# Half of the low-half subtractions of U moved from VectorE to GpSimd in the last expert stage

## The reference, cut to what matters

```python
def chunk(args):
    xc, ic, gc = args
    u = jnp.take(u_tab, ic, axis=0)
    act = jax.nn.gelu(jnp.einsum('chkd,cd->chk', u, xc), approximate=False)
    return jnp.einsum('chk,chkd->cd', gc * act, jnp.take(v_tab, ic, axis=0))
```

## Time and profile before

| | us |
|---|---|
| median of 3 runs | 2609.61 (2608.39 to 2610.11) |
| the profiled execution, device time | 2614.08 |
| span of its profile, first to last instruction | 2612.3 |
| PE busy | 2377.7 (91%) |
| DVE busy | 1766.5 (68%) |
| POOL busy | 908.3 (35%) |
| ACT busy | 777.9 (30%) |

### The profile page before, as it was taken

How to read it: one execution, slowest core, us unless ns; L and a number is a source line. 1 busy time by engine, 2 the same in 40 slices (tenths; PEclk the granted TensorE clock), 3 DMA queues, 4 the chain that set the end, 5 groups by cost and what they waited for, 6 DMA issues and landing times.

```text
span 2612.3 us, 34126 instructions
## 1 busy us (share of the span) xinstructions
PE 2377.7 (91%) x12686; PEld 1830.0 (70%) x12686; DVE 1766.5 (68%) x3612; ACT 777.9 (30%) x1388; POOL 908.3 (35%) x650
## 2 busy tenths in 40 slices
PE   5988899969999999999978778998899999999995
PEld 4756689859757766666657567987795777666662
DVE  1345479978668777677754456897884886777775
ACT  2354442113225422122243444311231452222221
POOL 3400360431221154555444205217113114555552
PEclk7999989989999999999989888999899999999997
DMA  6455334886799899999934702279669998999993
GB/s 262 139 179 193 131 112 129 312 313 226 281 316 317 281 366 370 366 364 366 366 115 147 209 25 85 92 269 360 207 223 344 313 320 316 377 378 356 384 369 133
DMA packets 219907, 679.71 MB, mean 260 GB/s; under 512 B 32384, under 2 KB 63152, under 8 KB 219232
## 3 DMA queue, kind: packets, MB, share of 16 engines
q1 hardware_dynamic: 142912, 396.42, 43.2%
q0 software_dynamic: 76832, 281.11, 28.7%
HBM read 658.87 MB, written 18.56 MB: 259 GB/s over the span
## 4 chain that ended last, share of the span: by engine, by line
PE 60%; DVE 15%; DMA 13%; ACT 4%; issue 3%; POOL 3%; SPq 1%; ACTq 0%; DVEq 0%
PE ps L1056 15%; PE ps L737 9%; PE ps L739 9%; PE ps L738 9%; DMA ring<-in_u 8%; PE ps L1033 7%; DVE arena L2033 3%; POOL arena L655 3%; PE ps L1012 2%; PE ps L919 2%; DMA arena<-gelu_half 2%; DMA arena<-in_u_rows,arena 2%; PE ps L900 2%; DVE arena L1927 1%; ACT u_split L1324 1%
## 5 line engine op out<-in xcount | busy, mean ns | idle before, releaser
L1056 PE MATMUL ps<-ring,arena 128*128 128x512 f32 x1264 | 568.9, 595 | 20.7 <-DVE arena L1981 20.6
L655 POOL DMA_INDIRECT arena<-in_u_rows,arena x256 | 294.0, 1148 | 782.6 <-DVE arena L2014 598.3
L655 POOL DMA_INDIRECT arena<-in_v,arena x256 | 355.8, 1390 | 353.8 <-DVE arena L2014 168.3
L1033 PE MATMUL ps<-arena,ring 128*128 128x256 f32 x2048 | 457.6, 382 | 1.1 <-ACT arena L1279 0.6
L1033 PEld LDWEIGHTS ps<-arena,ring 128*128 128x128 f32 x2048 | 386.5, 191 | 53.2 <-issue 1.9
L1056 PEld LDWEIGHTS ps<-ring,arena 128*128 128x128 f32 x1264 | 231.4, 190 | 268.8 <-issue 268.2
L615 POOL TENSOR_TENSOR ring_lo<-ring,ring_hi 128x1024 fp32r<-128x1024 f32 x84 | 216.4, 2588 | 415.5 <-ACT ring_hi L1158 415.5
L2014 DVE CUSTOM_DVE_ANT_0 arena<-arena 128x1024 f32<-128x1024 f32 x256 | 310.8, 1221 | 47.9 <-DMA arena<-in_u_rows,arena 47.5
L2033 DVE SCALAR_TENSOR_TENSOR arena<-arena 128x1024 f32<-128x1024 f32 x254 | 325.7, 1282 | 15.3 <-DMA arena<-in_v,arena 1.2
L737 PE MATMUL ps<-xs_high,u_split 128*128 128x256 f32 x1024 | 335.4, 328 | 0.1
L2003 DVE TENSOR_TENSOR u_split<-ring,u_split 128x1024 fp32r<-128x1024 f32 x128 | 156.7, 1224 | 218.4 <-ACT u_split L1324 218.4
(11 more groups left out here) (245 smaller groups left out, 3549.1 us busy)
## 6 DMA issues: line engine op xcount, KB each, us to landing
ring<-in_u SPq DMA_DIRECT2D x256, 512.0 KB, 6.3
ring<-in_v SPq DMA_DIRECT2D x256, 512.0 KB, 5.9
ring<-in_w_mod SPq DMA_DIRECT2D x80, 512.0 KB, 4.2
ring<-in_w_in SPq DMA_DIRECT2D x36, 512.0 KB, 3.3
ring<-in_w_q SPq DMA_DIRECT2D x32, 512.0 KB, 3.2
gelu_half<-arena SPq DMA_DIRECT2D x120, 128.0 KB, 4.7
arena<-gelu_half SPq DMA_DIRECT2D x120, 128.0 KB, 4.7
arena<-in_w_mod SPq DMA_DIRECT2D x16, 512.0 KB, 19.8
```

The costliest lines, as they stand in the source:

```text
L655: pool.indirect_dma_start(row[at], None, table, bass.IndirectOffsetOnAxis(where[:, k:k + 1], axis=0)).then_inc(sem(f"row_in{at}"), 16)
L1033: ins = mm(hidden_bank(b), slot[c % RING][:, P * k:P * k + P], HFS[:, k, :], start=(k == 0), stop=(k == KC - 1))
L1056: ins = mm(ps[:, t + 3 * q, :], GL[:, b % GLS, P * t - P:P * t], slot[c % RING][:, 512 * q:512 * q + 512], start=(b == MIDDLE[0]), stop=(b ...
```

## The change

The low halves of blocks 67, 69, ..., 127 are made by POOL. These are 31 blocks in each layer and 62 in all; the even ones, and block 65, stay on DVE. POOL's gathers are counted by r from 0 to 255 in the order of use. If S is the number of the first row of step b - 3, in which DVE made the low half of block b, POOL now makes it directly ahead of gather S + 4. `BESIDE` holds this place for each block.

```diff
+SHARED = range(SPILL + 3, KEYS, 2)
+BESIDE = {}
+for b in SHARED:
+    BESIDE.setdefault(min(HALF + sum(len(d) + len(s) for d, s in LATE[:b - 3 - SPILL]) + 4, 2 * P - 1), []).append(b)
...
+            def low_u(l, b):
+
+                c = u_chunk(l, b)
+                pool.wait_ge(sem("us_hi"), since("us_hi", l) + b - SPILL + 1)
+                pool.tensor_tensor(u_half(b, 1), slot[c % RING], f32(u_half(b, 0)), ALU.subtract).then_inc(used(c % RING), 1)
+
             def experts(l):
...
+                    for b in BESIDE.get(r, ()):
+                        low_u(l, b)
                     gather(l, r)
...
-                    if b + 3 < KEYS:
+                    if b + 3 < KEYS and b + 3 not in SHARED:
                         low_u(b + 3)
```

## The result

The changed kernel takes 2654.43 us (median of 4 runs, 2650.91 to 2664.07), the kernel before 2609.00 beside it (4 runs). The ratio is 1.0183, with a 95% interval of 1.0162 to 1.0205: slower by 45 us, where 18 were forecast.

What follows compares the result with a forecast made beforehand. PE and the DMA engines were taken as nearly full. Terms 6 + 11 + 0 + 5 - 4 gave +18 us on the profiled 2614.08, so 2632.1, or a median of 2627.6 us; range 2601 to 2655.

Steps and rivals of the forecast that it cites:

- path through the rows: Two gathers behind POOL's subtraction leave later; PE waits 0.8 us with one such row in the next step, 2.9 with two.
- term 3: Product at the other 48 steps: no wait if landings are about 1 us shorter; 0 taken, other end 38 us.
- price of the port: Port shared by DVE and POOL: either engine waits for the other; 0.6 us charged per tight block, within term 1.
- term 1: Hidden and product at 11 tight odd blocks: later low half costs 13 us, lower end -10; +6 taken.
- term 2: Three-row steps after blocks 79, 91, 103, 115, both layers: late gathers delay the product 0 to 2.9 us each; +11 us.
- term 4: Block 127, end of each layer's stage: late last gather delays the last products 0 to 3.5 us per layer; +5 us.
- Term 5: Even blocks: DMA queues drain as PE spreads out, so their loads land sooner; -4 us, ends 0 and -10.
- heavier rival: Landings stay at 8 us and POOL's queue turns on itself through late rows; about 2655 to 2665 us, chance 0.2.

Runs made afterwards that it cites:

- no_low: Changed kernel with the odd low halves left out on both engines (ACT signals by an eight-column copy), POOL only fetching; 0.9937 of the kernel before.
- tied_reads: Changed kernel, odd low halves left out, ACT signalling hidden; POOL waits for ACT's high half, then subtracts finished tiles, 27 per layer; 1.0172 of the kernel before.
- place6: Changed kernel with POOL's subtraction two fetches further back, ahead of gather S + 6; 1.0075 of the kernel before.
- place8: Changed kernel with POOL's subtraction four fetches further back, ahead of gather S + 8; 1.0425 of the kernel before.
- write_only3: Changed kernel with POOL filling the odd low halves with zeros three times (2.9 us, no reads) instead of subtracting; 1.0126 of the kernel before.
- doubles_dve: Changed kernel with blocks 79, 91, 103, 115 and 127 given back to DVE; 1.0186 of the kernel before.
- write_only: Changed kernel with POOL filling the odd low halves with zeros twice (1.9 us, no reads) instead of subtracting; 1.0019 of the kernel before.

## Why the prediction was right or wrong

**The bound and the sign** were right. PE and DMA were the nearly full resources, the win was capped by PE's idle time (20.7 us at best; no_low took 16), and the order on POOL did decide.

**The step that failed is "path through the rows", with term 3**, and with it the price of the port. The path let a row be used in 1.28 us and the product follow in 0.42, and counted 0 for 48 steps, because landings would fall to about 7. They fell to 7.1, so the reason given was right; the time of the two DVE instructions was not. With the measured 3.69 in the same sum, the outer product can start at U + 12.58 - 0.9 + 2.41 = U + 14.1, and PE gets there at U + 11.76: late by 2.3 us, where 0 was taken. That is an estimate: in the turn shown PE's recorded stop is 1.36 us at the outer product, and hidden waits in it too. The ends given for the term, 0 and 38, came from landings alone. What the held DVE cost is shown at equal time on POOL: 38 us, give or take 11.

Sorted by the prediction's terms, by where PE stood in the two stages against before, the 48.4 us are about: hidden 10.2 (term 1: 6); the product at the steps of term 2, 12.9 (11); the end of the stage 0 (term 4: 5); the product at all other steps, 10.6 (terms 3 and 5: -4); and PE's longer busy time, 14.5, which the prediction did not price. The last two are the gap. The sorting tells where PE stood, not what a term is worth alone, as term 2 shows.

**The port** was priced on one engine. The prediction had both numbers, five POOL subtractions of 3.33 and six DVE additions of 3.10 us each, and wrote that either waits for the other. But the sum charged only POOL's later start, 0.6 us in term 1. POOL's group gained 0.09 us in the mean, and DVE's rows 0.25 in the mean over all 254, up to 2.9 (a use of 4.15 us in layer 1) where the row was on the chain. The rule of the Trainium skill (page "SBUF — State Buffer", section Who interferes with whom) that the two lock each other out if GpSimd reads, and not if it only writes, agrees with the runs: 1284 ns beside fills, 1444 to 1535 beside subtractions. The prediction had read it for POOL only.

**Term 1** (+6): hidden does wait, 10.2 us in both stages, but tied_reads loses as much without that path. It was clearly the larger of the two waits only where POOL's work came later or lasted longer (place6, place8, write_only3).

**Term 2** (+11) is seen in the trace, and still is no addend. PE's three longest waits for a product in layer 0 came at products 78 (3.73 us), 102 and 114, and the longest of layer 1 at 102 (3.79 us): the steps behind blocks 79, 103 and 115 that the term names, and longer than its 2.9 us. From the timeline:

```profile
1158.23 6.47 PE L1068 MATMUL ps<-ring,arena 128*128 128x512 f32 x8 [3.34 <-DVE arena L1993]
1245.12 5.37 PE L1068 MATMUL ps<-ring,arena 128*128 128x512 f32 x8 [3.14 <-DVE arena L1993]
```

The chain into product 102 goes through the second fetch behind the subtraction, as the term says, and through a held product besides:

```profile
1143.95 1.76 POOL arena L659
...
1146.02 8.28 DMA arena<-in_v,arena
...
1154.32 1.28 DVE arena L2045
1155.60 2.49 DVE arena L1993
```

At the term's eight products the waits add up to 14.1 us, 1.2 before; there was none at product 90, and next to none at 78 and 114 of layer 1. But doubles_dve, which gives these blocks back, does not get the time back: its waits there are 0.5 to 1.2 us, others take their place, and the outer product still waits 37.4 us in all. A stop that is taken away lets PE run into the next one.

**Term 4** (+5) is absent. The last fetch and the products that needed it, layer 0:

```profile
1316.38 1.21 POOL L659 DMA_INDIRECT arena<-in_v,arena  x1 [0.31 <-issue]
...
1321.95 2.67 DVE L2045 SCALAR_TENSOR_TENSOR arena<-arena 128x1024 f32<-128x1024 f32 x2 [0.87 <-DMA arena<-in_v,arena]
1324.55 0.76 DVE L1993 SCALAR_TENSOR_TENSOR arena<-arena 128x256 f32<-128x256 f32 x2
...
1327.25 3.60 PE L1068 MATMUL ps<-ring,arena 128*128 128x512 f32 x8
```

The last two rows were both used by 1324.6, so the row had landed within some 7 us; the products were done at 1325.31, and the last two outer products, at 1327.25 and next behind it, did not wait for them.

**Term 5** (-4) had the right reason: the U blocks' loads land in 7.1 us and DVE has less of its own to do. What it was worth alone was not measured apart from the floor.

**The heavier rival** named the right size and, in part, the right circle; the size is luck in part. Its condition was wrong: landings did not stay at 8 us, and fetches hardly stood blocked by row buffers (24.1 us in layer 0's stage, less than before). The ring closes through the U load and the late row's use.

## What to carry to other kernels

Price a shared port on both engines, and at the instruction that stands on a path: there nearly the whole of the other engine's operation was added here (2.4 us), however small its effect on the mean. An engine that issues fetches isn't free for arithmetic because it is idle; what is put in its queue delays each fetch behind it. Follow such a delay round to where it began and hold the sum of the turn against the bound's own pace (here 27.5 against 25.2 us). In this case a turn under that pace cost little against the kernel before (write_only, about 24.7 us by the same estimate, 1.0019), and one beyond it much more. And do not add up stops that stand on one path: taking some away, as doubles_dve did, moved the time to others.

## What was not expected of the hardware

The granted clock of PE was low behind some of the new stops. Windows around one of them, columns as above:

```profile
985.00:991.00 6.00, 2.89 (x25) 2.69 (x23) 4.53 (x3) 1.33 (x2) 2.64 (x2) 0.90 1.03 415
991.00:998.00 7.00, 6.38 (x12) 2.96 (x13) 5.22 (x7) 1.06 (x1) 4.19 (x5) 0.60 0.93 325
```

and the outer product in the second, from the timeline, with the stop ahead of it:

```profile
991.62 6.15 PE L1068 MATMUL ps<-ring,arena 128*128 128x512 f32 x8 [3.73 <-DVE arena L1993]
```

PE had stood still for 3.73 us; then the mean granted clock was 0.60, so most of the stretch was at the 1.2 GHz level, and eight matmuls took 6.15 us instead of 3.69. Four more on the chain are alike:

```profile
1158.23 6.49 PE ps L1068 x8
...
1245.12 5.37 PE ps L1068 x8
...
2448.84 6.29 PE ps L1068 x8
...
2492.15 5.12 PE ps L1068 x8
```

Against 3.69 the five lost 11 us together, most of the 14.5 by which PE's busy time grew. So such a stop cost PE more than its own length. Not each did: behind a stop of 3.25 us, at 2216.83, the eight matmuls took 3.67. The kernel before has one such place (5.37 us behind a stop of 2.74, product 97). The prediction had no term for it. No run took the clock's share apart from the stops that it followed.
